# A two-block network on one core: more places for the expert weights, and GpSimd's transfers begun by ScalarE

## What is computed

```python
# first expert layer: 64 experts of width 256, eight of them for each token, and one shared expert
s = sigmoid(hf @ w_router);  idx = top_k(s + b_router, 8)
y = sum over chosen e of  w[e] * ((silu(x @ we_gate[e]) * (x @ we_up[e])) @ we_down[e])
y = y + (silu(x @ ws_gate) * (x @ ws_up)) @ ws_down
# second expert layer: 32 experts of width 512, two of them for each token
y = sum over e of  combine[:, e] * ((silu(x @ w_g[e]) * (x @ w_u[e])) @ w_d[e])
```

## Time and profile before

| | |
|---|---|
| median of 3 runs | 1489.98 us (1489.52 to 1491.17) |
| the profiled execution, its own time | 1492.28 us |
| its span, first to last instruction | 1490.5 us |
| PE (TensorE) busy | 1192.4 us, 80% |
| DVE, ACT, POOL busy | 357.8, 190.1, 95.5 us |
| moved by the DMA engines | 507.72 MB, mean 341 GB/s |
| SyncE's transfers (q1) | 502.97 MB |
| GpSimd's transfers (q0, software) | 944 packets, 3.29 MB |
| ScalarE's transfers (q10) | 144 packets, 0.07 MB |
| chain that ended last | PE 53%, DMA 35%, DVE 8% |

### The profile page before, as it was taken

How to read it: one execution, slowest core, us unless ns; L and a number is a source line. 1 busy time by engine, 2 the same in 40 slices (tenths; PEclk the granted TensorE clock), 3 DMA queues, 4 the chain that set the end, 5 groups by cost and what they waited for, 6 DMA issues and landing times.

```text
span 1490.5 us, 21157 instructions
## 1 busy us (share of the span) xinstructions
PE 1192.4 (80%) x8936; PEld 623.4 (42%) x8936; DVE 357.8 (24%) x926; ACT 190.1 (13%) x385; POOL 95.5 (6%) x126
## 2 busy tenths in 40 slices
PE   4999898999998989989997999888554665655635
PEld 2764344555554545545555554445221221212201
DVE  1498644611111111111103054333000000000002
ACT  1210200511111111111113012012000000000001
POOL 2399000000000000000000000000000000000000
PEclk9999978999999999999999999997786877868878
DMA  9874994269999999999978322736999999999994
GB/s 336 303 312 160 400 410 193 113 244 397 420 420 419 420 420 420 420 420 420 420 330 309 125 113 113 308 142 235 430 427 428 425 428 428 427 428 429 427 425 179
DMA packets 73029, 507.72 MB, mean 341 GB/s; under 512 B 6870, under 2 KB 8118, under 8 KB 35172
## 3 DMA queue, kind: packets, MB, share of 16 engines
q1 hardware_dynamic: 71844, 502.97, 82.3%
q0 software_dynamic: 944, 3.29, 0.7%
q10 hardware_dynamic: 144, 0.07, 0.0%
HBM read 505.25 MB, written 1.06 MB: 340 GB/s over the span
## 4 chain that ended last, share of the span: by engine, by line
PE 53%; DMA 35%; DVE 8%; SPq 2%; issue 1%; ACT 1%; DVEq 0%; ACTq 0%
DMA W<-in_we_up 11%; DMA W<-in_w_expert_gate 8%; PE PS L1473 8%; PE PS L1645 5%; PE PS L1349 4%; PE PS L1484 4%; DMA W<-in_w_expert_down 4%; DMA W<-in_w_expert_up 4%; PE PS L1543 4%; PE PS L1336 3%; PE PS L982 2%; DMA W<-in_w_ada 2%; PE PS L1659 2%; DMA scr<-in_w_expert_up 2%; DMA hx<-in_w_expert_down 2%; DMA scr<-in_w_expert_down 2%
## 5 line engine op out<-in xcount | busy, mean ns | idle before, releaser
L1645 PE MATMUL PS<-W,scr 128*32 128x512 f32 x736 | 141.1, 709 | 119.1 <-DMA W<-in_w_expert_gate 78.2
L1473 PE MATMUL PS<-W,scr 128*32 128x256 f32 (+1 forms) x2752 | 189.1, 394 | 34.7 <-DMA W<-in_we_up 31.7
L2144 DVE TENSOR_TENSOR scr<-scr,PS 128x256 f32<-128x256 f32 (+1 forms) x33 | 23.5, 711 | 656.2 <-PE PS L1645 376.8
L1473 PEld LDWEIGHTS PS<-W,scr 128*32 128x32 f32 (+1 forms) x2752 | 115.4, 118 | 115.5 <-issue 65.7
L1645 PE MATMUL PS<-scr 128*32 128x512 f32 x208 | 115.2, 718 | 32.7 <-DMA W<-in_w_expert_up 32.7
L1349 PE MATMUL PS<-scr 128*128 128x512 f32 x264 | 122.1, 605 | 2.5 <-ACT scr L870 2.5
L1645 PEld LDWEIGHTS PS<-W,scr 128*32 128x32 f32 x736 | 36.4, 128 | 201.7 <-issue 157.1
L1336 PE MATMUL PS<-scr 128*128 128x128 bf16 x1584 | 95.3, 221 | 3.7 <-DVE scr L2125 3.7
L1336 PEld LDWEIGHTS PS<-scr 128*128 128x128 bf16 x1584 | 92.6, 99 | 5.5 <-issue 5.2
L859 ACT COPY scr<-PS 128x512 f32<-128x512 f32 x66 | 38.7, 587 | 435.5 <-PE PS L1336 435.5
L1484 PE MATMUL PS<-W,scr 128*32 128x512 f32 (+1 forms) x688 | 91.1, 596 | 0.7 <-DVE scr L2147 0.7
(11 more groups left out here) (417 smaller groups left out, 1275.5 us busy)
## 6 DMA issues: line engine op xcount, KB each, us to landing
W<-in_we_gate SPq DMA_DIRECT2D x64, 1024.0 KB, 19.2
W<-in_we_up SPq DMA_DIRECT2D x64, 1024.0 KB, 18.8
W<-in_we_down SPq DMA_DIRECT2D x64, 1024.0 KB, 21.5
W<-in_w_expert_gate SPq DMA_DIRECT2D x25, 2048.0 KB, 28.3
W<-in_w_expert_up SPq DMA_DIRECT2D x21, 2048.0 KB, 26.6
W<-in_w_ada SPq DMA_DIRECT2D x10, 4096.0 KB, 18.3
W<-in_w_expert_down SPq DMA_DIRECT2D x16, 2048.0 KB, 23.2
W<-in_w_in SPq DMA_DIRECT2D x5, 4096.0 KB, 14.8
```

The costliest lines, as they stand in the source:

```text
L1473: m = mm(PS[4 + kind][at:at + size, 0:F1], hTe[:, k, at:at + size], piece_view((g, kind, j))[:, k, :], start=(k == 0), stop=(k == KD - 1))
L1645: m = mm(PS[4 + kind][j * CAP2:(j + 1) * CAP2, :], hTe[:, k, j * CAP2:(j + 1) * CAP2], piece_view2((g, kind, j))[:, k, :], start=(k == 0), ...
L2144: v.tensor_tensor(av[:, 0:F].rearrange("s (c p) -> s p c", p=P), sg[:, 0:F].rearrange("s (p c) -> s p c", p=P), PS[5][:, 0:F].rearrange("s ...
```

## The change

It has three parts that belong together.

1. The eight transfers that GpSimd began are begun by ScalarE, at the places of ScalarE's stream where their conditions hold: the gain rows behind the fourth root (wait `hn_ready`), the router's weights ahead of the first `root_of` (waits `gates_made` and `mixT_conv`), the four at `x2_ready` behind the second layer's first modulation, and `rowf` ahead of the second `experts`. GpSimd begins none. The area for its descriptor ring is asked for with 1024 bytes, and the scratch area `scr` grows by 3840 words in each partition (15,360 bytes).
2. The first expert layer gets 17 places: the 12 slots, three places of 1 MB at the end of `scr`, one in `xn` ("rows") and one in `hT` ("features"). Piece i goes to place i mod 17; pieces 12 to 16 wait for nothing, for `branch_in` 4 and `ada_summed` 7 (twice), for `hs_part` and `hs_left` 8, and for the shared expert's gate and up. TensorE waits once for each set (a group's gates, ups or downs), no longer once for each piece. `ring_free` looks at the last 17 pieces.
3. The second expert layer gets ten places of 2 MB; four are filled at `attn_done` in place of three.

The core of the diff:

```diff
-SLOTS, SLOT_WORDS, RING0 = 12, 2048, 0
+SLOTS, SLOT_WORDS = 12, 2048
+
+PLACES1 = list(range(12)) + ["scratch2", "scratch0", "scratch1", "rows", "features"]
 PIECES1 = [(-1, kind, 0) for kind in range(3)] + [(g, kind, j) for g, group in enumerate(GROUPS1) for kind in range(3) for j in range(len(group))]
-RING = {piece: ((RING0 + i) % SLOTS, i // SLOTS) for i, piece in enumerate(PIECES1)}
-RING_USES = [sum(slot == s for slot, _ in RING.values()) for s in range(SLOTS)]
-
-
-PLACES2 = [5, 4, 6, 0, 1, 2, 3, 7, 8]
+RING = {piece: PLACES1[i % len(PLACES1)] for i, piece in enumerate(PIECES1)}
+
+SETS1 = [(-1, kind) for kind in range(3)] + [(g, kind) for g in range(NG1) for kind in range(3)]
+SET_SIZE = [1 if g < 0 else len(GROUPS1[g]) for g, _ in SETS1]
+LANDED1 = {m: sum(SET_SIZE[i] for i in range(n % 12, n + 1, 12)) for n, m in enumerate(SETS1)}
+assert min(sum(SET_SIZE[n:n + 12]) for n in range(len(SETS1) - 11)) > len(PLACES1)
+RING_USES = [sum(SET_SIZE[n::12]) for n in range(12)]
+
+
+PLACES2 = [5, 4, 6, 7, 0, 1, 2, 3, 8, 9]
...
-        NS = 14784
+        NS = 18624
...
+        spare1 = {"scratch0": scr[:, NS - 3 * SLOT_WORDS:NS - 2 * SLOT_WORDS], "scratch1": scr[:, NS - 2 * SLOT_WORDS:NS - SLOT_WORDS],
+                  "scratch2": scr[:, NS - SLOT_WORDS:NS], "rows": xn[:].rearrange("p a b -> p (a b)"), "features": hT_words}
+
         def slot_words(piece):
-            s = RING[piece][0]
-            return W[:, s * SLOT_WORDS:(s + 1) * SLOT_WORDS]
+            s = RING[piece]
+            return W[:, s * SLOT_WORDS:(s + 1) * SLOT_WORDS] if s in range(SLOTS) else spare1[s]
 
         def piece_view(piece):
             return slot_words(piece).rearrange("p (k n) -> p k n", k=F1 // P if piece[1] == 2 else KD)
-        assert NS - 3 * SLOT_WORDS >= SPARE2, SPARE2
-        afar = {6: scr[:, NS - 3 * SLOT_WORDS:NS - SLOT_WORDS], 7: scr[:, NS - SLOT_WORDS:NS + SLOT_WORDS], 8: hx[:, 0:2 * SLOT_WORDS]}
+        assert NS - 5 * SLOT_WORDS >= SPARE2, SPARE2
+        afar = {6: scr[:, NS - 3 * SLOT_WORDS:NS - SLOT_WORDS], 7: scr[:, NS - 5 * SLOT_WORDS:NS - 3 * SLOT_WORDS],
+                8: scr[:, NS - SLOT_WORDS:NS + SLOT_WORDS], 9: hx[:, 0:2 * SLOT_WORDS]}
...
-                slot = RING[piece][0]
-                if i >= SLOTS:
-                    consumed(PIECES1[i - SLOTS])
+                place = RING[piece]
+                if i >= len(PLACES1):
+                    consumed(PIECES1[i - len(PLACES1)])
+                elif place == "scratch2":
+                    pass
+                elif place in ("scratch0", "scratch1"):
+                    sp.wait_ge(S["branch_in"], 4)
+                    sp.wait_ge(S["ada_summed"], 7)
+                elif place == "rows":
+                    sp.wait_ge(S["hs_part"], 8)
+                    sp.wait_ge(S["hs_left"], 8)
+                elif place == "features":
+                    sp.wait_ge(S["sh_gateup"], NB)
                 else:
 
-                    sp.wait_ge(S["stream_used"], AT[("adb4", "adb5", "w_out")[slot // 4]] + 1)
+                    sp.wait_ge(S["stream_used"], AT[("adb4", "adb5", "w_out")[place // 4]] + 1)
...
-                sp.dma_start(piece_view(piece), src).then_inc(S[f"ring{slot}"], 16)
+                sp.dma_start(piece_view(piece), src).then_inc(S[f"ring{SETS1.index(piece[0:2]) % 12}"], 16)
...
-                for piece in PIECES1[-SLOTS:]:
-                    if RING[piece][0] in slots:
+                for piece in PIECES1[-len(PLACES1):]:
+                    if RING[piece] in slots:
...
-            fill((5, 4, 6))
+            fill((5, 4, 6, 7))
             sp.wait_ge(S["stream2_used"], 5)
             fill((0, 1))
             sp.wait_ge(S["stream2_used"], 6)
             fill((2, 3))
             sp.wait_ge(S["backT"], 8)
-            fill((7,))
+            fill((8,))
             sp.wait_ge(S["hs_part"], 16)
             sp.wait_ge(S["hs_left"], 16)
-            fill((8,))
+            fill((9,))
...
-            pool.wait_ge(S["hn_ready"], 1)
-            for name, src in (("post_mix", A["g_post_mix"][0]), ("post_ffn", A["g_post_ffn"][0])):
-                pool.dma_start(rowd[name], src.partition_broadcast(P)).then_inc(S["rowd_loaded"], 16)
-
-            pool.wait_ge(S["gates_made"], 1)
-            pool.wait_ge(S["mixT_conv"], 4)
-            pool.dma_start(wr, A["w_router"][0].rearrange("(p k) n -> p k n", k=KD)).then_inc(S["wr_loaded"], 16)
...
-            pool.wait_ge(S["backT"], 8)
-            pool.dma_start(rowf, A["norm_f_g_2"].partition_broadcast(P)).then_inc(S["poolw_loaded"], 16)
...
+            act.wait_ge(S["hn_ready"], 1)
+            for name, src in (("post_mix", A["g_post_mix"][0]), ("post_ffn", A["g_post_ffn"][0])):
+                act.dma_start(rowd[name], src.partition_broadcast(P)).then_inc(S["rowd_loaded"], 16)
...
+            act.wait_ge(S["gates_made"], 1)
+            act.wait_ge(S["mixT_conv"], 4)
+            act.dma_start(wr, A["w_router"][0].rearrange("(p k) n -> p k n", k=KD)).then_inc(S["wr_loaded"], 16)
...
+            act.wait_ge(S["x2_ready"], 1)
+            act.dma_start(TBr, bass.AP(bias_dram.tensor, 0, [[1, P], [T + P - 1, HEADS2], [1, T]])).then_inc(S["bias_loaded"], 16)
+            act.dma_start(poolw, A["pool_w_2"][0].rearrange("g c d -> c g d")).then_inc(S["poolw_loaded"], 16)
+            for dst, name in ((wr2[:, :, 0:4], "w_router_group_2"), (wr2[:, :, 4:36], "w_router_expert_2")):
+                act.dma_start(dst, A[name][0].rearrange("(p k) n -> p k n", k=KD)).then_inc(S["wr_loaded"], 16)
...
+            act.wait_ge(S["backT"], 8)
+            act.dma_start(rowf, A["norm_f_g_2"].partition_broadcast(P)).then_inc(S["poolw_loaded"], 16)
...
-            def landed(piece):
-
-                slot, turn = RING[piece]
-                pe.wait_ge(S[f"ring{slot}"], 16 * (turn + 1))
+            def landed(g, kind):
+
+                pe.wait_ge(S[f"ring{SETS1.index((g, kind)) % 12}"], 16 * LANDED1[g, kind])
...
-    nc = bacc.Bacc("TRN2", target_bir_lowering=False, num_devices=1)
+    nc = bacc.Bacc("TRN2", target_bir_lowering=False, num_devices=1, dynamic_dma_scratch_size=1024)
```

More of the change, by code:

```diff
@@ L418, in two_block_network @@
         w_o = wv["w_out"].rearrange("p (k n) -> p k n", k=KD)
-        sh_gu = W[:, RING0 * SLOT_WORDS:(RING0 + 2) * SLOT_WORDS].rearrange("p (c k n) -> p c k n", c=2, k=KD)
+        sh_gu = W[:, 0:2 * SLOT_WORDS].rearrange("p (c k n) -> p c k n", c=2, k=KD)
         sh_dn = piece_view((-1, 2, 0))
@@ L702, in _ @@
                     step(g.tensor_tensor(acc, acc, tmp, ALU.add), S["conv_ready"] if j == taps - 1 else None)
-            pool.wait_ge(S["hn_ready"], 1)
-            for name, src in (("post_mix", A["g_post_mix"][0]), ("post_ffn", A["g_post_ffn"][0])):
-                pool.dma_start(rowd[name], src.partition_broadcast(P)).then_inc(S["rowd_loaded"], 16)
-            pool.wait_ge(S["gates_made"], 1)
-            pool.wait_ge(S["mixT_conv"], 4)
-            pool.dma_start(wr, A["w_router"][0].rearrange("(p k) n -> p k n", k=KD)).then_inc(S["wr_loaded"], 16)
-            pool.wait_ge(S["x2_ready"], 1)
-            pool.wait_ge(S["stored"], 16)
-            pool.dma_start(TBr, bass.AP(bias_dram.tensor, 0, [[1, P], [T + P - 1, HEADS2], [1, T]])).then_inc(S["bias_loaded"], 16)
-            pool.dma_start(poolw, A["pool_w_2"][0].rearrange("g c d -> c g d")).then_inc(S["poolw_loaded"], 16)
-            for dst, name in ((wr2[:, :, 0:4], "w_router_group_2"), (wr2[:, :, 4:36], "w_router_expert_2")):
-                pool.dma_start(dst, A[name][0].rearrange("(p k) n -> p k n", k=KD)).then_inc(S["wr_loaded"], 16)
             pool.wait_ge(S["tb_flipped"], 4)
@@ L1443, in shared_down @@
                 last.then_inc(S["sh_turned"], 1)
-                landed((-1, 2, 0))
+                landed(-1, 2)
                 pe.wait_ge(S["hs_left"], 4)
@@ L1454, in _ @@
             for kind in range(2):
-                landed((-1, kind, 0))
+                landed(-1, kind)
             pe.wait_ge(S["gates_made"], 2)
@@ L1468, in gate_and_up1 @@
                 for kind in range(2):
-                    for j in range(len(GROUPS1[g])):
-                        landed((g, kind, j))
+                    landed(g, kind)
                     for k in range(KD):
@@ L1477, in down1 @@
             def down1(g):
-                for j in range(len(GROUPS1[g])):
-                    landed((g, 2, j))
+                landed(g, 2)
                 for c in range(F1 // P):
```

## The result

The changed kernel takes 1473.39 us (median of four runs, 1471.51 to 1476.18), the kernel before 1490.58 (four runs beside it). The ratio is 0.9883, 95% interval 0.9867 to 0.9900: 1.2% faster. Forecast were 1472.5 us, with a range of 1470.0 to 1479.5.

The account below looks back on a forecast made before the run. The prediction took both expert layers to be bound by transfers, with DMA engines idle ahead of them. Leads of 12.6 and 4.9 us sum to 17.5, from a median of 1489.98 to 1472.5 us, range 1470 to 1479.5.

Parts of the forecast that it names:

- What bounds it: Both expert layers' flat stretches: bound by transfers, the second by a wide margin, the first only just; DMA idle ahead of each.
- The unit and the first layer's term: First expert layer: a piece costs 2.52 us, five more are loaded ahead, so the last lands 12.6 us earlier.
- Does TensorE follow?: First expert layer: TensorE has waited 31.7 us, so the whole 12.6 us arrives and about 19 us of waits remain.
- rival B: First expert layer: TensorE becomes the bound and part of the lead is lost; 1478.8 us if half goes, chance 0.09.
- The second layer's term: Second expert layer: one more piece begun early, in the window of DMA share 0.53, gains 4.9 us.
- Between the layers: Second mixer: its first item is begun some 12 us sooner but gains 0, since transposes wait 7.64 us for VectorE.
- ScalarE begins eight transfers: ScalarE's queue, four places: beginning the moved transfers is covered by idle time and costs 0.
- top price: Beginning a transfer: 8.77 us at most, from SyncE's bias row behind two transfers of many short rows.
- C: Both expert layers: only one lead counts, 1477.4 us with 12.6 alone or 1485.1 with 4.9 alone; chance 0.08.
- D: Flat stretches lose rate as pieces land in buffers in use, 1496.1 us at 395 GB/s in the first layer; chance 0.05.
- E: SyncE's queue is held at a new wait and one ScalarE transfer costs 4.8 us; 1487 to 1492 us, chance 0.04.
- (b): Ahead of the first expert layer: ScalarE begins the router's weights with 4 us of cover; 0, or 4.8 us late at worst.

Follow-up runs that it names:

- e4: The changed kernel with 17 places, but piece 12 and all behind it wait until the first group's gates are used; 1489.97 us, ratio to before 0.9997.
- e2: The changed kernel, but the second expert layer keeps nine places; 1479.80 us, ratio to the kernel before 0.9930.
- e6: The changed kernel, but only the first half of each first-layer down matrix is loaded from the third group on; 1442.34 us, ratio 0.9689.
- e3: The changed kernel, but the first expert layer keeps 12 places; 1487.82 us, ratio to the kernel before 0.9985.

## Why the prediction was right, point by point

- *What bounds it.* Right. Both flat stretches kept their rate, and what was gained was gained by bytes moved ahead of them. e4 shows it for the first layer: the same ring without the early bytes takes 3.5 us longer than before, not 12.9 less.
- *The unit and the first layer's term*, 5 x 2.52 = 12.6 us: 12.9 in the profiles of the changed kernel and before, 12.6 between their second ones, 13.0 in e2. The times at which new places come free were read from rows, and all came out where they were read, less the 2.0 to 3.4 us by which the execution ran ahead.
- *Does TensorE follow?* Yes, but the reserve was mis-sized. I wrote "about 19 us of waits are left as the next bound", from a row of the waits for ups alone; three waits for gates, 2.6 us, stand beside it. The waits left are 24.1 us, 21.6 of them for ups: they shrank by 10.2, not by the 12.6 of the lead, because 2.4 us of the gain are shorter multiplications. The sign that they shrink "by about the lead" is met only loosely. And the distance to TensorE's own bound is 34 us (e6), because the waits go with a lower granted clock, and that loss stands in no row of waits. The row of waits was read as if it held the whole cost. It did no harm, since the error makes rival B less likely than the 0.09 I gave it.
- *The second layer's term*, 4.9 us: 5.1 to 5.2 (e3, and the changed kernel). Its size was right, its place was not: I put the extra piece's transfer into the window with a DMA share of 0.53, 1020 to 1040 us, but it is moved right behind `attn_done`, where the share rose from 0.85 to 1.01.
- *Between the layers*, 0. The first item of the second mixer was begun 11.7 us ahead of the last downs' end (759.73 against 771.41). It gained nothing, as forecast: the mixer's first multiplication came 17.1 us behind that end (788.52), as before (804.71 behind 787.60), behind transposes that waited the same 7.64 us for VectorE:

```profile
784.85 3.84 PE L1265 MATMUL PS<-ident,hx 128*128 128x128 f32 x16 [7.64 <-DVE hx L2055]
```

- *ScalarE begins eight transfers*, 0. In the profile it is right in all four places, in the medians up to some 2.5 us are open (above); its timeline around the first three:

```profile
233.21 0.36 ACTq L821 DMA_DIRECT2D scr<-in_g_post_mix  x1
233.60 0.81 ACTq L821 DMA_DIRECT2D scr<-in_g_post_ffn  x1
246.19 0.40 ACT L754 COPY modc<-PS 128x48 f32<-128x48 f32 x3 [15.89 <-PE PS L1010]
252.72 0.34 ACTq L911 DMA_DIRECT2D scr<-in_w_router  x1
256.88 0.63 ACT L833 ACTIVATE hx<-hx 128x512 f32<-128x512 f32 x1 [10.29 <-DVE hx L2203]
```

Each costs 0.34 to 0.81 us, near GpSimd's 0.75; the router's weights are begun at 252.72 and ScalarE's next work at 256.88 waits for VectorE as before. At `x2_ready`:

```profile
788.73 0.38 ACTq L937 DMA_DIRECT2D scr<-bias_by_distance  x1
...
789.15 0.60 ACTq L938 DMA_DIRECT2D scr<-in_pool_w  x1
...
789.78 0.64 ACTq L940 DMA_DIRECT2D scr<-in_w_router_group  x1
790.45 2.57 ACTq L940 DMA_DIRECT2D scr<-in_w_router_expert  x1
793.06 1.28 ACT L946 ACT_TABLE_LOAD   x1 [3.13 <-issue]
856.05 0.40 ACT L946 ACTIVATE scr<-scr,small 128x128 f32<-128x128 f32 x1 [61.71 <-DVE small L2270]
```

The last of these, the expert router's matrix in many short rows, held ScalarE's queue for 2.57 us; the first exponential comes at 856.05. `rowf` took 0.35 us at 1002.21, and ScalarE's copy after it waited 7.76 us for TensorE, 7.77 before. Nothing came near the top price of 8.77 us. Neither of the two multiplications named as signs came late: VectorE's was at 251.28 (254.59 less the 3.3 us of this execution) and TensorE's at 843.61 (860.24 less 16.6, the 3.3 and the first layer's lead). From issue to landing (KB, us) the bias took 5.6 us where GpSimd's took 10.7, the second gain row 6.7, as before:

```profile
scr<-bias_by_distance ACTq DMA_DIRECT2D x1, 1024.0 KB, 5.6
...
scr<-in_g_post_ffn ACTq DMA_DIRECT2D x1, 512.0 KB, 6.7
```

- *The sum.* 17.5 us were forecast; the span shows 18.6, the medians 17.2, and 15.1 when both were run again. That the span shows more than the forecast is the 0.6 us by which the two terms were larger and 0.5 in the rest: the start of the first layer (-3.3) against the end (+1.7) and the stretch to the second layer (+1.1). So the median's closeness to the forecast, 17.2 against 17.5, is in part luck: the leads came out 0.6 us larger, and the medians fall short of the leads by 0.9 us here and 2.6 in the repeat.
- *The rivals.* B is refuted by e6 (34 us of room), C by e2 and e3, D by the slices, whose rate did not move with five of 17 places in `scr`, `xn` and `hT`; E by the queue's rows and by (b), begun at 252.72 with nothing behind it late. D's measure for wrong, 412 GB/s, was never neared.
- *The disagreement with the page's figure* (the Trainium skill, DMA: Bandwidth & Descriptors, section "Where 436 GB/s comes from", 358 GB/s from HBM): the piece cost 12.9 / 5 = 2.6 us, against 2.93 by the page and 2.52 by the period. The trace was the better guide.

## What to carry to other kernels

Where a stretch runs at the rate of the transfers, look for the idle DMA time ahead of it and count the bytes that can be moved there: each is worth its time at the flat rate. Buffers that can't be filled in that time bring none of this, only what they save of gaps within the stretch (here some 4 us). Buffers that are dead at that moment (a norm's rows, a transposed copy, the end of the scratch area) serve as places for a few pieces, and releasing half a place when half of its use is done gave 3.5 us more for a few lines. Check with one run that takes the transfers away how far the compute engine is from being the bound: the sum of its waits falls short.

## What the runs showed of the hardware that I had not expected

- TensorE's waits understate what it loses: 25.6 us idle went with 8.9 us of longer multiplications, and with no waits for transfers (e6) the granted clock was 1.00 over 428 us.
- Beginning a transfer has no single price: 0.33 us for 1 MB in long rows on SyncE's queue, 2.57 us for a matrix of short rows on ScalarE's, 8.49 us (8.77 before) for one row copied to all partitions behind two transfers on SyncE's.
- Profiles of kernels with the same work differ by about 5 us up to the first expert layer (307.7 to 313.0) and by 1.7 us at the end, where the last 32 multiplications take 3.69 us at a granted clock of 1.00 or 5.38 at 0.76. Differences of 0.1 to 0.3% are safer read from the stretch that a change touches than from the total.
